# Who splits the last two query tiles of a layer into high and low parts: ScalarE and VectorE, or GpSimd

## The reference, cut to what matters

```python
def trunk_layer(x, cond, ctx_k, ctx_v, p):
    h = rms_norm(x, p['norm1_g']) * (1.0 + sc1) + sh1
    q, k, v, u = mixer_projections(h, p['w_in'], p['q_norm_g'], p['k_norm_g'])
    ...
        cos, sin = axial_rope_tables(x.shape[1])
        q = apply_axial_rope(q, cos, sin)
        k = apply_axial_rope(k, cos, sin)
    ...
    attn = block_attention(q, keys, vals)      # softmax(q k^T / 8) v per head
    pooled = pool_mixer(u, p['w_pool'], p['pool_scale'])
    mix = jnp.concatenate([attn, pooled], axis=-1) @ p['w_out']
    x = x + gt1 * mix
    h2 = rms_norm(x, p['norm2_g']) * (1.0 + sc2) + sh2
    x = x + gt2 * conv_ffn(h2, p['w_up'], p['conv_w'], p['conv_b'], p['w_down'])
```

## Time and profile before

| | us |
|---|---|
| median of 3 runs | 1446.1 (1445.47 to 1446.18) |
| profiled execution, its own time | 1448.74 |
| its span, first to last instruction | 1446.9 |
| busy in the span: TensorE matmuls | 1413.3 (98%) |
| VectorE | 905.7 (63%) |
| ScalarE | 536.6 (37%) |
| GpSimd | 390.5 (27%) |

### The profile page before, as it was taken

The page is one execution under the profiler, slowest core; times in us unless marked ns, Lnnn a source line. Parts: engine busy times, 40 slices in busy tenths (PEclk is TensorE's granted clock), DMA queues, the critical chain, the costliest instruction groups (busy, mean ns, idle before and its releaser), DMA issues.

```text
span 1446.9 us, 25120 instructions
## 1 busy us (share of the span) xinstructions
PE 1413.3 (98%) x9945; PEld 1359.0 (94%) x9945; DVE 905.7 (63%) x1429; ACT 536.6 (37%) x802; POOL 390.5 (27%) x265
## 2 busy tenths in 40 slices
PE   6998999999999999999999999999999999999997
PEld 4887889999999999999999977999999999999997
DVE  4548869897976478785775887269844323444333
ACT  5436862533231123332242687244232112332322
POOL 0263002143530024434214700213433101323321
PEclk9999999999999999999999999999999999999999
DMA  9752005253435234434423200124322322222321
GB/s 317 242 180 79 2 2 153 81 160 116 156 122 167 93 106 145 127 120 149 124 58 86 63 1 2 59 88 132 101 72 85 90 59 74 73 72 72 101 61 74
DMA packets 198159, 147.05 MB, mean 102 GB/s; under 512 B 4401, under 2 KB 187449, under 8 KB 197049
## 3 DMA queue, kind: packets, MB, share of 16 engines
q1 hardware_dynamic: 196592, 144.27, 32.4%
q10 hardware_dynamic: 1480, 1.57, 0.3%
HBM read 142.94 MB, written 2.88 MB: 101 GB/s over the span
## 4 chain that ended last, share of the span: by engine, by line
PE 87%; DVE 8%; ACT 2%; issue 2%; SPq 1%; DMA 1%; DVEq 0%; ACTq 0%
PE pair L1442 68%; PE pair L1458 7%; PE pair L1835 3%; PE pair L1878 3%; PE pair L1849 2%; DVE mod_acc L1034 2%; DVE in_lo L1100 1%; DVE norm_t L1090 1%; DVE conv L1364 1%; SPq L409 1%; DVE small L1312 1%; DVE w_lo L1011 1%; PE pair L1742 1%; DMA w_first<-in_w_mod_dram 1%; PE pair L1694 1%
## 5 line engine op out<-in xcount | busy, mean ns | idle before, releaser
L1442 PE MATMUL pair<-in_hi,w_hi 128*128 128x384 f32 x1728 | 395.5, 310 | 1.5 <-DVE w_lo L1011 1.4
L1442 PE MATMUL pair<-in_lo,w_hi 128*128 128x384 f32 x1728 | 395.1, 310 | 0.0
L1442 PE MATMUL pair<-in_hi,w_lo 128*128 128x384 f32 x1728 | 392.8, 308 | 0.0
L1364 DVE SCALAR_TENSOR_TENSOR conv<-pair,vec,conv 128x127 f32<-128x127 f32 x352 | 168.7, 541 | 194.6 <-ACT conv L919 194.1
L1442 PEld LDWEIGHTS pair<-in_hi,w_hi 128*128 128x128 f32 x1728 | 265.1, 189 | 6.6 <-DVE w_lo L1011 2.0
L1442 PEld LDWEIGHTS pair<-in_lo,w_hi 128*128 128x128 f32 x1728 | 265.4, 189 | 0.0
L1442 PEld LDWEIGHTS pair<-in_hi,w_lo 128*128 128x128 f32 x1728 | 263.8, 188 | 0.0
L618 POOL TENSOR_TENSOR silu_a<-silu_a,conv 128x640 f32<-128x640 f32 x44 | 111.8, 2540 | 536.8 <-DVE conv L1364 536.8
L919 ACT ACTIVATE conv<-pair,vec 128x640 f32<-128x640 f32 x88 | 77.8, 886 | 408.9 <-PE pair L1442 406.7
L1011 DVE TENSOR_TENSOR w_lo<-w_raw,w_hi 128x1024 fp32r<-128x1024 f32 (+1 forms) x148 | 197.7, 1336 | 37.6 <-ACT w_hi L640 37.2
L640 ACT ACTIVATE w_hi<-w_raw 128x1024 fp32r<-128x1024 f32 (+1 forms) x82 | 97.0, 1183 | 302.8 <-PE pair L1442 286.1
(11 more groups left out here) (202 smaller groups left out, 1784.5 us busy)
## 6 DMA issues: line engine op xcount, KB each, us to landing
w_raw<-in_w_up_dram SPq DMA_DIRECT2D x88, 512.0 KB, 3.7
mod_raw<-in_w_mod_dram SPq DMA_DIRECT2D x64, 512.0 KB, 4.1
w_raw<-in_w_down_dram SPq DMA_DIRECT2D x32, 704.0 KB, 4.6
w_raw<-in_w_in_dram SPq DMA_DIRECT2D x20, 512.0 KB, 4.0
w_first<-in_w_mod_dram SPq DMA_DIRECT2D x16, 512.0 KB, 8.8
w_raw<-in_w_out_dram SPq DMA_DIRECT2D x16, 512.0 KB, 4.1
mod_raw<-in_w_mod_dram SPq DMA_DIRECT2D x4, 1024.0 KB, 4.9
mod_acc<-in_w_mod_dram SPq DMA_DIRECT2D x4, 1024.0 KB, 4.9
```

The source lines that it names most:

```text
L1364: ins = dve.scalar_tensor_tensor(out=conv[:, s, d0:d1], in0=up_result(g, j, s)[:, d0 + sh:d1 + sh], scalar=v(L, V_TAP[t], s * NF + g * FG ...
L1442: ins = pe.matmul(dst[:, a:e], w[:, s, k, :], rhs[:, kk, a:e], start=first and r == 0, stop=last and r == 2)
```

## The change

For the query tiles 3 and 4 the split goes to GpSimd, which does it right behind the rotation of the same tile: high part of the first head, its low part, high part of the second, its low part, with a wait between each two. Only then does it rotate the next tile. ScalarE's and VectorE's copies of those steps in the attention loop go. Tiles 1 and 2 stay as they were. TensorE waits for heads 4 to 7 on a new semaphore, `s_qp`, that GpSimd posts; the counts of `s_qs` are made for two tiles (`NS` = 2) instead of four.

```diff
@@ gpsimd, behind the rotation of tile e
                     pool.tensor_tensor(tgt, tgt, rope[:, 1, :], ALU.add).then_inc(s_qk, 1)
+                    if e > NS:
+
+                        pool.wait_ge(s_qk, E + 1)
+                        for i in range(2):
+                            a, o = i * HALF, (1 - i) * HALF
+                            H = 2 * (L * (NQ - NS) + e - 1 - NS) + i
+                            pool.tensor_copy(q_st[a:a + HALF, 2 * (e - 1) + i, :], qk[a:a + HALF, e % 3, :]).then_inc(s_qp_hi, 1)
+                            pool.wait_ge(s_qp_hi, H + 1)
+                            pool.tensor_tensor(q_st[o:o + HALF, 2 * (e - 1) + i, :], qk[a:a + HALF, e % 3, :],
+                                               q_st[a:a + HALF, 2 * (e - 1) + i, :].bitcast(F32),
+                                               ALU.subtract).then_inc(s_qp, 1)
+
+                            pool.wait_ge(s_qp, H + 1)
...
@@ scalar, attention loop
-                        if i in (0, 1):
-                            q_hi(3, (i,))
-                        if i in (3, 4):
-                            q_hi(NQ, (i - 3,))
...
@@ vector, attention loop
-                    if i in (2, 3):
-                        q_low(3, (i - 2,))
-                    if i in (4, 5):
-                        q_low(NQ, (i - 4,))
...
@@ tensor, scores
-                    pe.wait_ge(s_qs, 2 * L * NQ + h + 1)
+                    if h < 2 * NS:
+                        pe.wait_ge(s_qs, 2 * L * NS + h + 1)
+                    else:
+                        pe.wait_ge(s_qp, 2 * L * (NQ - NS) + h - 2 * NS + 1)
```

More of the change, by code:

```diff
@@ L293, in build @@
         s_qs_hi, s_qs, s_ks_hi, s_ks = sem("query_hi"), sem("query_split"), sem("key_hi"), sem("keys_split")
+        s_qp_hi, s_qp = sem("late_query_hi"), sem("late_query_split")
+        NS = NQ - 2
         s_first, s_const0 = [sem(f"first_loaded{i}") for i in range(8)], sem("ident_loaded")
@@ L797, in q_std, with q_hi @@
                                      scale=1.0 / (HD * SCALE ** 2)).then_inc(s_qsd, 1)
-                def q_hi(e, heads=(0, 1)):
+                def q_hi(e):
                     act_e.wait_ge(s_qk, L * NE + e + 1)
-                    for i in heads:
+                    for i in range(2):
                         a = i * HALF
@@ L824, in _ @@
                         elif e > 3:
-                            act_e.wait_ge(s_qs, 2 * (L * NQ + e - 3))
+                            act_e.wait_ge(s_qs, 2 * (L * NS + e - 3))
                         if e == 0:
@@ L1245, in shuffle, with q_low @@
                     dve.stream_shuffle(rope[:, 0, :], latent, [(i + 16) % 32 for i in range(32)]).then_inc(s_shuf, 1)
-                def q_low(e, heads=(0, 1)):
-                    for i in heads:
+                def q_low(e):
+                    for i in range(2):
                         a, o = i * HALF, (1 - i) * HALF
-                        dve.wait_ge(s_qs_hi, 2 * (L * NQ + e - 1) + i + 1)
+                        dve.wait_ge(s_qs_hi, 2 * (L * NS + e - 1) + i + 1)
                         dve.tensor_tensor(q_st[o:o + HALF, 2 * (e - 1) + i, :], qk[a:a + HALF, e % 3, :],
```

## The result

The changed kernel takes 1449.3 us (median of 11 runs, 1448.4 to 1450.3) against 1446.1 for the kernel before on the same chip: ratio 1.002, 95% interval 1.0012 to 1.0028. On another chip, beside the experiments, it was 1448.9 against 1446.8, ratio 1.0014 (1.0004 to 1.0024). So it is slower, by 2 to 3 us; the prediction had 1 us. The mechanism that the prediction priced is there, nearly to the tenth. A second one, TensorE's clock, was not in it at all.

A forecast was written before the change was run, and what follows sets the result against it. VectorE was taken to pace units 3 to about 8, TensorE the rest. Removing 3.5 us a layer against waits of 3.05 and 4.65 us left +0.2 and -1.2: 1.0 us slower, 1447.1 from 1446.1; range 1442.9 to 1450.5.

The forecast's parts named there:

- The mechanism that the prediction priced: Early attention loop: VectorE instructions wait for the end of GpSimd's, 3.05 us in layer 0 and 4.65 in layer 1.
- The removal: VectorE's four low parts a layer go: 3.5 us a layer taken away, 2.35 arriving, 4.7 in both.
- GpSimd's instructions: Added split on GpSimd: copy 0.72 us, subtraction 1.56, with 0.17 before each; 5.2 us a tile.
- The third rival: GpSimd's added split is slower than its nearest rows: 5.4 us slower, 1451.5; chance 0.15.
- TensorE's new wait: TensorE's wait for heads 4 to 7 ends no stretch; the last head has more than 3 us to spare.
- Which forms wait: VectorE's small product and scaling wait for GpSimd in the loop; the maximum and reciprocal don't.
- The first and second rivals: VectorE in the loop: only the scaling waits, 1.4 us faster, chance 0.15; or waits hardly matter, 1441.4, chance 0.12.
- The sum of the waits: VectorE's products and scalings in the early units: 3.05 us in layer 0, 4.65 in layer 1.
- Their net effect: Removal less waits: 0.2 us gained in layer 0, 1.2 lost in layer 1, 1.0 us slower in sum.
- the part on the price: GpSimd and VectorE working together at the loops' start: mutual waits of 3.05 and 4.65 us.
- from unit 8 on everything is TensorE's and simply moves: Attention loop after the early units: TensorE sets the pace, 2.04 us a unit, so earlier shifts carry through unchanged.
- the line of 0.2%: Whole kernel: 2.9 us tells a change from none; within 0.69, faster by more 0.13, slower by more 0.18.

The follow-up runs named there:

- e5: Changed kernel with seven more spare multiplications behind unit 1's scores and six ahead of unit 4's; median +1.1 us against the kernel before, ratio 1.0002.
- e9: Changed kernel unaltered, run again; median +2.1 us against the kernel before, ratio 1.0004 to 1.0024.
- e6: Kernel before with the small product as one tensor times a scalar per partition; median +1.1 us, ratio 0.9996 to 1.0014.
- e8: Kernel before with the scaling of the probabilities of units 0 to 3 on ScalarE; median +0.4 us, ratio 0.9994 to 1.0012.

## Why the prediction was right and wrong

- **The removal**: 4.7 us in both layers predicted; measured 2.5 us in the layer that nothing disturbed, 3.7 in both loops, 4.1 in the median.
- **GpSimd's instructions**: taken as the undisturbed rows of the MLP's, 0.72 and 1.56 us; they are 0.71 and 1.54. The third rival falls. TensorE's new wait ends no stretch, as predicted. The spaces between dependent instructions were taken at 0.17 us and are 0.08; so the queue ends 134.8 - 130.5 = 4.3 us behind the first maximum and not 136.6 - 131.5 = 5.1, and in layer 1 8.9 us behind it and not 10.0.
- **Which forms wait**: the product and the scaling do, the maximum and the reciprocal don't, and each wait ends with GpSimd's instruction. The first and second rivals fall. The earlier trace rows carried this: two instructions of eight columns had foretold one of one column.
- **The sum of the waits**: 3.05 us in layer 0 and 4.65 in layer 1 predicted. Measured, each instruction less its undisturbed length: 1.37 + 0.38 + 1.31 = 3.1 and 1.01 + 0.83 + 1.02 + 1.09 + 1.10 = 5.05. Which ones was wrong in part: the third in layer 0 was a scaling and not unit 2's product, and layer 1 had two waiting products, not four, and the scalings of units 0, 1 and 2. The prediction had said that tenths decide; it is hundredths.
- **Their net effect**: scores of unit 8 at 13.7 and 14.9 us; with the clock held at 2.4 GHz, 13.55 and 15.01 (e5). The predicted 1.0 us net came out as 0.9, and layer by layer 0.2 gained and 1.2 lost as 0.3 and 1.2. That it fits so closely where other instructions waited than foretold is in part luck. The third rival's 5.4 us was added up on another base: it sets its waits of 4.5 + 5.6 us against the 2.35 us a layer that arrive, the forecast against the 3.5 taken away, by which the rival would be 3.1 us slower.
- **What failed** is the part on the price. It followed the delay of VectorE into the next scores, and stopped at "from unit 8 on everything is TensorE's and simply moves". It never asked what a longer wait does to TensorE itself. The kernel before puts spare multiplications into TensorE's waits, which leaves 0.64 and 0.94 us idle before units 2 and 4 of layer 0; with the same number the change leaves 2.02 and 1.55 us, in layer 1 1.18 and 1.60. That is 2.9 of the 3.8 us in the loops of the first profile; layer 0, counted at 0.2 us gained, lost 1.9. In e9's profile, with smaller waits and 10.2 us at half clock, the loops lost only 1.7 us, so the clock's share differs from one execution to the next.
- The time fell inside the range, in its upper part, and for another reason than the one that the range had been opened for. The ratio's interval, 0.12% to 0.28%, lies across the line of 0.2%.

## What to carry to other kernels

Work moved to an idle GpSimd is paid by VectorE, instruction by instruction, when both touch SBUF at one time; before moving it, try the form with one tensor input for VectorE's smallest operations (it freed the product of one column here, while the scalings of 128 and 640 columns still waited). VectorE's maxima, which read PSUM, took as long beside GpSimd as alone (0.28 and 0.82 us), so work beside them should cost nothing; no run moved it there. Where a kernel keeps TensorE busy with spare work, its amount belongs to one schedule: after any edit upstream, read TensorE's idle times and granted clock again. And judge a change of this size by the distance between two points of the stretch that it touches, since one profiled execution holds 1 to 2 us of luck in other places; and take that distance from more than one execution, since it differed by 2.1 us between two profiles of the changed kernel (+3.8 and +1.7).

## What the runs showed of the hardware that I had not expected

A VectorE product of 128 x 1 waited 1.37 us for a GpSimd instruction that started 0.01 us ahead of it, and not at all when it started 0.01 us behind the product. The same product with its second input as a scalar for each partition takes 0.21 us beside GpSimd and alone, against 0.16. And TensorE's clock fell to 1.2 GHz for 6.8 us inside a kernel that keeps it busy for 98% of the span, around idle stretches of 2.0 and 1.6 us in layer 0 and of 1.2 and 1.6 us in layer 1; with only one of the two left it fell for 3.4 us or, in layer 1 with the second filled, not at all. Its price was anything from nothing (e6 and e8, 3.4 us) to 2.2 us (6.8 us in layer 0).
